# Loading weight slabs in pairs: one 512 KB transfer where two 256 KB slabs belong to one output tile

## The reference

```
h = x + 0.5 * post1(swiglu(pre1(x), ffn1_w_in, ffn1_w_out))     # 1024 -> 2 x 2816 -> 1024
z = pre_mix(h) @ w_in                                           # 1024 -> 42 x 128
A = differential attention(z);  B = RWKV-7 time mixing(z)
m = sigmoid(gA) * (A @ w_o_att) + sigmoid(gB) * (B @ w_o_rwkv)
h = h + post_mix(m @ w_out)
y = h + 0.5 * post2(swiglu(pre2(h), ffn2_w_in, ffn2_w_out))
```

## Time and profile before

| | |
|---|---|
| median of three runs | 4056.09 us (4051.56 to 4056.75) |
| the profiled execution | 4052.75 us, its span 4051.0 us |
| PE busy | 3431.7 us (85% of the span) |
| DVE, ACT, POOL busy | 1953.4, 1326.0 and 326.0 us |
| loads through the `raw` rings | 660 in `front`, 504 in `back`; 256 KB each, 48 of them 128 KB |
| mean DMA rate over the span | 116 GB/s |

### The profile page before, as it was taken

One profiled execution on the slowest core, in us unless ns is written; L12 is line 12 of the kernel. 1 busy time (PEld: TensorE's weight loads), 2 busy tenths in 40 slices (PEclk: granted clock), 3 DMA queues, 4 the chain that ended last, 5 costly groups with the idle time before them and its releaser, 6 DMA issues. The chain is left out here.

```text
span 4051.0 us, 64534 instructions
## 1 busy us (share of the span) xinstructions
PE 3431.7 (85%) x26233; PEld 3148.7 (78%) x26233; DVE 1953.4 (48%) x3180; ACT 1326.0 (33%) x2363; POOL 326.0 (8%) x483
## 2 busy tenths in 40 slices
PE   3999999999997977848635999985789979997995
PEld 3999999999997965524314888874689969996995
DVE  3446444564445436652395323315465465556543
ACT  2345344443433322321122111111344434343432
POOL 0000110001000120000131111102000010000000
PEclk7999999999998988979767989986889989998998
DMA  4445554455544541034301000002534544554444
GB/s 156 126 139 152 165 168 128 145 157 173 146 126 132 172 166 47 1 126 183 144 24 42 3 3 3 3 14 81 164 112 126 165 149 124 150 155 134 126 127 171
DMA packets 652371, 468.63 MB, mean 116 GB/s; under 512 B 34085, under 2 KB 619601, under 8 KB 649906
## 3 DMA queue, kind: packets, MB, share of 16 engines
q1 hardware_dynamic: 630914, 392.52, 31.9%
q0 software_dynamic: 21168, 71.97, 5.1%
HBM read 400.63 MB, written 63.77 MB: 115 GB/s over the span
## 5 line engine op out<-in xcount | busy, mean ns | idle before, releaser
L495 DVE TENSOR_TENSOR fr_wlo<-fr_raw,fr_whi 128x512 fp32r<-128x512 f32 (+1 forms) x660 | 449.9, 682 | 733.8 <-ACT fr_whi L403 733.8
L403 ACT ACTIVATE fr_whi<-fr_raw 128x512 fp32r<-128x512 f32 (+1 forms) x660 | 410.0, 623 | 776.2 <-PE ps L631 747.2
L855 DVE TENSOR_TENSOR bk_wlo<-bk_raw,bk_whi 128x512 fp32r<-128x512 f32 x504 | 341.9, 678 | 481.1 <-ACT bk_whi L767 480.9
L631 PE MATMUL ps<-fr_hidhi,fr_whi 128*128 128x384 f32 x1536 | 514.8, 335 | 0.0
L631 PE MATMUL ps<-fr_hidlo,fr_whi 128*128 128x384 f32 x1536 | 513.6, 334 | 0.0
L631 PE MATMUL ps<-fr_hidhi,fr_wlo 128*128 128x384 f32 x1536 | 513.6, 334 | 0.0
L767 ACT ACTIVATE bk_whi<-bk_raw 128x512 fp32r<-128x512 f32 x504 | 312.1, 619 | 528.5 <-PE ps L1007 495.6
L1007 PE MATMUL ps<-bk_xahi,bk_whi 128*128 128x384 f32 x1248 | 425.3, 341 | 52.9 <-DVE bk_xalo L927 42.1
L1007 PE MATMUL ps<-bk_xalo,bk_whi 128*128 128x384 f32 x1248 | 420.2, 337 | 0.0
L1007 PE MATMUL ps<-bk_xahi,bk_wlo 128*128 128x384 f32 x1248 | 420.0, 337 | 0.0
L631 PE MATMUL ps<-fr_xahi,fr_whi 128*128 128x384 f32 x1056 | 357.8, 339 | 13.6 <-DVE fr_xalo L564 12.7
(11 more groups left out here) (383 smaller groups left out, 5213.0 us busy)
## 6 DMA issues: line engine op xcount, KB each, us to landing
fr_raw<-in_ffn_w_in_dram SPq DMA_DIRECT2D x264, 256.0 KB, 2.9
bk_raw<-in_ffn_w_in_dram SPq DMA_DIRECT2D x264, 256.0 KB, 2.9
fr_raw<-in_w_in_dram SPq DMA_DIRECT2D x252, 256.0 KB, 2.9
fr_raw<-in_ffn_w_out_dram SPq DMA_DIRECT2D x120, 256.0 KB, 2.8
bk_raw<-in_ffn_w_out_dram SPq DMA_DIRECT2D x120, 256.0 KB, 2.8
zT_scratch<-fr_zo POOLq DMA_DIRECT2D x126, 192.0 KB, 2.7
sa_kc<-in_cache_att_k_dram SPq DMA_DIRECT2D x8, 2048.0 KB, 11.7
sa_vc<-in_cache_att_v_dram SPq DMA_DIRECT2D x8, 2048.0 KB, 7.4
```

What stands on the lines that cost most here:

```text
L403: act.activation(w["hi"][:, s % RING, 0:x.n], raw[:, s % RING, 0:x.n], ACT.Copy).then_inc(whi, 1)
L495: dve.tensor_tensor(w["lo"][:, s % RING, 0:x.n], raw[:, s % RING, 0:x.n], w["hi"][:, s % RING, 0:x.n].bitcast(F32), ALU.subtract).then_inc ...
L631: ins = pe.matmul(ps[:, b, 0:NN], w[wt][:, x.s % RING, k], rhs(xt, x.k0 + k), start=f, stop=l)
L855: dve.tensor_tensor(w["lo"][:, s % RING, 0:x.n], raw[:, s % RING, 0:x.n], w["hi"][:, s % RING, 0:x.n].bitcast(F32), ALU.subtract).then_inc ...
```

## The change

Two slabs that follow each other in the list become a pair when the first has an even number, both belong to the same unit, both are full, and their blocks follow each other in the weight matrix. A pair is loaded by one DMA of 8 blocks into two neighbouring slots of `raw`. SP issues it when the second of the two slots is free: when `wlo` of slab `s - 3` has been formed, `s` being the first of the pair. Both slabs count as landed with the one completion, which `arrival` tells to ACT. All else, also the rings of four and the split three slabs ahead, stays.

```
+    def first(self, x):
+        y = self.slabs[x.s + 1] if x.s + 1 < len(self.slabs) else None
+        return x.s % 2 == 0 and y is not None and y.unit == x.unit and x.n == y.n == KS and y.k0 == x.k0 + KS
...
             for x in plan.slabs:
-                if x.s >= RING:
-                    sp.wait_ge(wlo, x.s - RING + 1)
+                if plan.second(x):
+                    continue
+                both = plan.first(x)
+                n, last = (2 * KS, x.s + 1) if both else (x.n, x.s)
+                if last >= RING:
+                    sp.wait_ge(wlo, last - RING + 1)
...
-                sp.dma_start(raw[:, x.s % RING, 0:x.n], src).then_inc(raw_in[x.s % RING], 16)
+                q = x.s % RING
+                dst = raw[:, q:q + 2].rearrange("p q k c -> p (q k) c") if both else raw[:, q, 0:n]
+                sp.dma_start(dst, src).then_inc(raw_in[q], 16)
...
-                act.wait_ge(raw_in[s % RING], 16 * (s // RING + 1))
+                act.wait_ge(raw_in[plan.arrival[s][0]], plan.arrival[s][1])
```

More of the change, by code:

```diff
@@ L270, in __init__, with second @@
         self.ended = {i: x for i, x in enumerate(slots) if x is not None and x.last}
+        self.arrival = []
+        issued = [0] * RING
+        for x in self.slabs:
+            if self.second(x):
+                self.arrival.append(self.arrival[-1])
+            else:
+                issued[x.s % RING] += 1
+                self.arrival.append((x.s % RING, 16 * issued[x.s % RING]))
+    def first(self, x):
+        y = self.slabs[x.s + 1] if x.s + 1 < len(self.slabs) else None
+        return x.s % 2 == 0 and y is not None and y.unit == x.unit and x.n == y.n == KS and y.k0 == x.k0 + KS
+    def second(self, x):
+        return x.s % 2 == 1 and self.first(self.slabs[x.s - 1])
     def end(self, kind, third, tile):
@@ L354, in _ @@
             for x in plan.slabs:
-                if x.s >= RING:
-                    sp.wait_ge(wlo, x.s - RING + 1)
+                if plan.second(x):
[4 more added lines that the diff above has]
+                    sp.wait_ge(wlo, last - RING + 1)
                 cols = slice(x.tile * P, (x.tile + 1) * P)
                 if x.kind == "g":
-                    src = w_up[:, x.k0:x.k0 + x.n, cols]
+                    src = w_up[:, x.k0:x.k0 + n, cols]
                 elif x.kind == "u":
-                    src = w_up[:, x.k0:x.k0 + x.n, FF + x.tile * P:FF + (x.tile + 1) * P]
+                    src = w_up[:, x.k0:x.k0 + n, FF + x.tile * P:FF + (x.tile + 1) * P]
                 elif x.kind == "d":
-                    src = w_down[:, x.k0:x.k0 + x.n, cols]
+                    src = w_down[:, x.k0:x.k0 + n, cols]
                 else:
-                    src = w_z[:, x.k0:x.k0 + x.n, cols]
-                sp.dma_start(raw[:, x.s % RING, 0:x.n], src).then_inc(raw_in[x.s % RING], 16)
+                    src = w_z[:, x.k0:x.k0 + n, cols]
+                q = x.s % RING
+                dst = raw[:, q:q + 2].rearrange("p q k c -> p (q k) c") if both else raw[:, q, 0:n]
+                sp.dma_start(dst, src).then_inc(raw_in[q], 16)
         @block.gpsimd
@@ L711, in _ @@
             for x in plan.slabs:
-                if x.s >= RING:
-                    sp.wait_ge(wlo, x.s - RING + 1)
+                if plan.second(x):
+                    continue
+                both = plan.first(x)
+                n, last = (2 * KS, x.s + 1) if both else (x.n, x.s)
+                if last >= RING:
+                    sp.wait_ge(wlo, last - RING + 1)
                 c0 = x.tile * P + (FF if x.kind == "u" else 0)
-                src = w_of["g" if x.kind == "u" else x.kind][:, x.k0:x.k0 + x.n, c0:c0 + P]
-                sp.dma_start(raw[:, x.s % RING, 0:x.n], src).then_inc(raw_in[x.s % RING], 16)
+                src = w_of["g" if x.kind == "u" else x.kind][:, x.k0:x.k0 + n, c0:c0 + P]
+                q = x.s % RING
+                dst = raw[:, q:q + 2].rearrange("p q k c -> p (q k) c") if both else raw[:, q, 0:n]
+                sp.dma_start(dst, src).then_inc(raw_in[q], 16)
         @block.gpsimd
```

## The result

The median is 4061.93 us (20 runs, 4053.85 to 4074.56) against 4052.53 us before (20 runs, 4046.54 to 4058.77). The ratio is 1.0023 with a 95% interval of [1.0015, 1.0031]: +9.4 us, slower by just over what the measurement tells from no change. The forecast was 4061.5, its sum +7.2. The profiled execution took 4069.75 us, its span 4068.0.

The account below looks back on a forecast made before the run. PE was taken to bound the dense stretches, with loads hidden except in a few places. Terms 3.2 + 0.6 + 2.3 + 1.6 - 0.5 = +7.2 us on the 4054.3 us mean of four executions gave 4061.5 us, range 4054 to 4071.

Parts of the forecast that it names:

- Steady stretches: Dense stretches: a pair lands in 3.8 us, 1.0 us before ACT's split needs it; cost nothing.
- The start of `front`, +3.2: Stage start: third slab counts as landed with the fourth, at 55.6 instead of 52.4; +3.2 us, lower bound nothing.
- The first start of `post`, +0.6: Near 356 us: pair lands 0.86 us later behind the residual load, moving the chain about one split; +0.6 us.
- The second start, 0: Start of `post` one third later: first split moves 0.9 us, but the next waits for PE until 816.15; nothing.
- The down tiles in `back`, +2.3 and +1.6: Second down tile, first and second third: slab 126's pair and its later counterpart land late; PE waits 2.3 and 1.6 us.
- Gates, -0.5: Gate loads, three thirds: pairs move out of some loads' way and into others'; -0.5 us, bounds minus 2 and plus 1.5.
- The clock, kept out of the sum as a rival: Slow clock after new PE gaps at 356, 3154, 3536 costs 1.7 us each: +12.3 in all, 4066.6; chance 0.26.
- the waits in the down tiles: Sign of being right: PE waits for `wlo` of 2.3 us and 1.6 in `back`'s second down tile, first two thirds.
- the third split near 52 us: Sign of being wrong at the start of `front`: ACT's third split near 52 instead of about 55.6.
- a clock below 1.00 behind new gaps: Sign of being wrong: PE's granted clock falls below 1.00 after the new gaps.
- The rival *faster: Gate loads gain some 8 us of their 20.1 us of waits, the start loses nothing: 4049 us; chance 0.06.

Follow-up runs that it names:

- crowded_only: Only the 12 pairs around `post`'s start in `front` and the second down tile in `back`, all else single; against the kernel before: 1.0018 [1.0006, 1.0029].
- uncrowded: All pairs except those 12 around `post`'s start in `front` and the second down tile in `back`, loaded singly; against the kernel before: 0.9993 [0.9981, 1.0004].

## Why the prediction was right, and where it was not

**Steady stretches: right.** The row of 180 to 225 us did not change, pairs land in the 3.8 us that the sum used, and 480 pairs without the twelve crowded ones cost nothing that can be seen (0.9993). Only where the `o` tiles begin, which the sum left out, did ACT come to wait for its slabs, and PE's wait there (`bk_hidlo`) is 15.4 us for 14.8.

**The start of `front`, +3.2: the step that failed.** It said that "the queue holds the same bytes in the same order", so the pair would count when the fourth slab used to. In the two queues together the order is not the same. Two issues bring in 1 MB where four were needed, and it enters before POOL's packets. DMA queues from 1.7 to 5.7 us after SP's first issue, first of the kernel before (46 to 50 us), then of the changed one (47.63 to 51.63):

```profile
q1 hardware_dynamic: 1421, 0.71, 62.8%
q0 software_dynamic: 130, 0.48, 38.6%
```

```profile
q1 hardware_dynamic: 1899, 0.96, 87.0%
q0 software_dynamic: 64, 0.29, 21.8%
```

Over the traces, the third split comes 7.7, 8.1, 9.1 and 10.1 us after SP's first issue with single loads (the earlier trace rows is the 8.1), and 6.4 to 7.1 in nine traces with pairs; PE's first sum 14.0 to 16.5 us, and 12.7 to 13.4. The term is -2.0 (between the medians, 14.9 and 13.0), not +3.2; the lower bound of nothing was not low enough.

**The first start of `post`, +0.6: right in size.** The gap is 2.45 for 1.72, +0.7. This rests on two traces; where the residual load is whole, six traces with pairs at this place have 2.03 to 2.94 us, and four with single slabs have 2.06, 1.72, 0.25 and none, so the term may be larger.

**The second start, 0: wrong.** The second split's wait for PE hid when its slab landed: anywhere up to 816.15. ACT's wait for the load grew from 1.15 to 3.14 us, and PE's gap from 0.35 to 2.34: +2.0, and 1.7 of slow clock behind it. The gap of the kernel before:

```profile
816.40 0.91 PE L637 MATMUL ps<-fr_ny,ones 128*128 128x384 f32 x2 [0.35 <-DVE fr_ny L527]
```

**The down tiles in `back`, +2.3 and +1.6: right.** 2.32 and 1.47 us, in that place and for that reason: `crowded_only` has them, `uncrowded` has not, and they go when POOL's loads are apart.

**Gates, -0.5: not shown.** DVE's wait went from 20.1 to 19.2, but PE's wait behind it from 10.8 to 11.5. Over the traces DVE waits 19.2 to 22.1 us with pairs in `back` and 18.4 to 21.2 without.

**The clock, kept out of the sum as a rival: half true.** 14 of the 16 PE gaps of 2.0 to 2.9 us at these places, over seven traces (one of them, 2.06 us, with single slabs), were followed by a granted clock of 0.50 to 0.66 in 4 us; two (2.03 and 2.45 us) by 1.00, as were all four of 1.4 to 1.5 us and that of 1.72. In the changed kernel that is 1.7 + 1.4 = 3.1 us, about the size of two of the rival's three stretches; one of them lies where the rival had it (behind the second down tile), the other at the second `post`, where the sum had no gap at all.

The Trainium skill (TensorE: Matmul & The Clock Gate, HAM oscillation) says that waits for DMA between groups of matmuls make the engine restart at the slow clock; the waits of its example are longer than these gaps. The 14 gaps agree with it, the two that kept 1.00 do not.

Of the signs that the prediction named, the waits in the down tiles came as it said, but so did two of its signs of being wrong: the third split near 52 us and a clock below 1.00 behind new gaps. (The rival *faster* does not add up either: 4054.3 + 0.6 + 2.3 + 1.6 - 8 is 4050.8, not 4049; nothing else hangs on it.)

So the total came out near the forecast by luck, because two errors met: the start was 5.2 us too high (3.2 against -2.0), and the second `post` and the clock were 2.0 + 3.1 = 5.1 too low. A third met them: the sum was added to 4054.3 us, 1.8 above the median of the kernel before, which hid most of the 2.2 us by which +7.2 falls short of +9.4. With the errors put right the sum stays at about +7, inside the +6.1 to +12.6 us that the interval of the ratio allows; what fills the rest to +9.4, if anything, is not settled.

## What to carry to other kernels

In this kernel larger loads cost nothing that could be seen where they land before ACT and PE need them, and what they cost came from the few places where another queue filled the DMA engines at the same time. List those places first; here one of them, where the `o` tiles begin, was missed. Add to a PE gap of 2 to 3 us in a dense stretch 1.4 to 2.0 us for the slow clock behind most of them: (1 - 0.66) x 4 to (1 - 0.50) x 4. Where two queues meet, ask which one's bytes are in first: the same bytes in fewer issues can be there sooner. The simpler cure was to issue the other queue's loads a few slabs apart: with that, all pairs cost nothing that could be told (1.0002). And a version that edits two things at once needs the control that has only one of them.

## What was not expected of the hardware

Beside POOL's loads, SP's queue with its 512-byte packets got 0.18 MB in 4 us while POOL's with packets of 3.9 KB got 1.27, and in the 2 us before, with SP's pair already issued, it got nothing. Loads on POOL's queue kept packets of 3.4 to 3.9 KB though their rows were cut to 512 bytes. And PE gaps of nearly one length gave both clocks: 1.00 after 2.45 us, 0.57 after 2.34.
